# 64 unused bytes in front of the activation tiles: every operand tile of the dense matmuls moves by 64 bytes

## What is computed

```python
x = x + 0.5 * ((silu(h @ w_gate) * (h @ w_up)) @ w_down)      # three times, 1024 x 2816 each
z = h @ w_in + b_in                                            # 1024 x 6672
merged = gates[0] * (attn @ w_proj_attn) + gates[1] * (mlstm @ w_proj_mlstm)
x = x + merged @ w_out
proj = h @ w_in_2                                              # 1024 x 1968
h = h + concat(o_gla, o_mla) @ w_out_2
h = h + (cross attention of h over mem) @ xa_w_o
```

## Time and profile before

| | us |
|---|---|
| median of 3 runs | 1047.71 (1047.59 to 1049.11) |
| profiled execution | 1046.08 |
| its span, from first to last instruction | 1044.4 |
| TensorE (PE) busy | 1011.0, 97% |
| VectorE (DVE) busy | 690.8, 66% |
| ScalarE (ACT) busy | 538.4, 52% |
| GpSimd (POOL) busy | 102.2, 10% |

### The profile page before, as it was taken

The page is one execution under the profiler, slowest core; times in us unless marked ns, Lnnn a source line. Parts: engine busy times, 40 slices in busy tenths (PEclk is TensorE's granted clock), DMA queues, the critical chain, the costliest instruction groups (busy, mean ns, idle before and its releaser), DMA issues.

```text
span 1044.4 us, 20581 instructions
## 1 busy us (share of the span) xinstructions
PE 1011.0 (97%) x8317; PEld 992.4 (95%) x8317; DVE 690.8 (66%) x1084; ACT 538.4 (52%) x779; POOL 102.2 (10%) x66
## 2 busy tenths in 40 slices
PE   6999999999999899999999999999989989999998
PEld 5999999998999799999999999999979889999998
DVE  5766665466869958766666636595566467787642
ACT  4554444244557964455444555485545555444431
POOL 1111110000000100001111104100001012222100
PEclk8999999999999999999999999999999999999999
DMA  8556665554553444565656654344235264655851
GB/s 248 180 178 186 198 221 167 177 162 131 159 196 121 145 138 140 182 223 182 193 168 189 218 193 125 116 123 153 89 104 159 62 202 149 190 184 172 261 171 41
DMA packets 168492, 172.33 MB, mean 165 GB/s; under 512 B 5604, under 2 KB 166894, under 8 KB 168302
## 3 DMA queue, kind: packets, MB, share of 16 engines
q1 hardware_dynamic: 165262, 170.57, 51.4%
q10 hardware_dynamic: 3168, 0.88, 0.5%
HBM read 170.39 MB, written 1.06 MB: 164 GB/s over the span
## 4 chain that ended last, share of the span: by engine, by line
PE 83%; DVE 6%; ACT 5%; issue 4%; DMA 1%; POOL 1%; SPq 0%; ACTq 0%; DVEq 0%; POOLq 0%
PE acc L655 76%; DVE wl L462 2%; DMA raw<-in_ffn_w_gate 1%; ACT wh L443 1%; POOL sq L2545 1%; PE part L992 1%; ACT L1395 0%; PE part L732 0%; PE part L708 0%; PE part L1191 0%; ACT prob L1334 0%; PE part L982 0%; ACT prob L1561 0%; PE part L780 0%; PE part L1173 0%
## 5 line engine op out<-in xcount | busy, mean ns | idle before, releaser
L443 ACT ACTIVATE wh<-raw 128x1024 fp32r<-128x1024 f32 (+3 forms) x298 | 319.4, 1095 | 317.0 <-PE acc L655 189.9
L655 PE MATMUL acc<-ah,wh 128*128 128x256 f32 x1520 | 436.0, 287 | 12.1 <-DVE al L1753 4.1
L462 DVE TENSOR_TENSOR wl<-raw,wh 128x1024 fp32r<-128x1024 f32 (+3 forms) x298 | 391.0, 1351 | 75.8 <-ACT wh L443 72.4
L655 PE MATMUL acc<-ah,wl 128*128 128x256 f32 x1520 | 431.9, 284 | 0.0
L655 PE MATMUL acc<-al,wh 128*128 128x256 f32 x1520 | 431.8, 284 | 0.0
L655 PEld LDWEIGHTS acc<-ah,wh 128*128 128x128 f32 x1520 | 290.1, 191 | 17.5 <-issue 6.9
L655 PEld LDWEIGHTS acc<-ah,wl 128*128 128x128 f32 x1520 | 290.1, 191 | 0.0
L655 PEld LDWEIGHTS acc<-al,wh 128*128 128x128 f32 x1520 | 290.0, 191 | 0.0
L655 PE MATMUL acc<-hh,wh 128*128 128x256 f32 x528 | 148.7, 282 | 0.0
L655 PE MATMUL acc<-hh,wl 128*128 128x256 f32 x528 | 148.6, 281 | 0.0
L655 PE MATMUL acc<-hl,wh 128*128 128x256 f32 x528 | 148.6, 281 | 0.0
(11 more groups left out here) (391 smaller groups left out, 1290.8 us busy)
## 6 DMA issues: line engine op xcount, KB each, us to landing
raw<-in_ffn_w_gate SPq DMA_DIRECT2D x33, 1024.0 KB, 5.3
raw<-in_ffn_w_up SPq DMA_DIRECT2D x33, 1024.0 KB, 5.3
raw<-in_ffn_w_down SPq DMA_DIRECT2D x24, 1408.0 KB, 6.4
raw<-in_w_in SPq DMA_DIRECT2D x33, 1024.0 KB, 5.3
raw<-in_w_out SPq DMA_DIRECT2D x8, 1024.0 KB, 5.2
raw<-in_w_proj_attn SPq DMA_DIRECT2D x4, 1024.0 KB, 5.1
raw<-in_w_proj_mlstm SPq DMA_DIRECT2D x4, 1024.0 KB, 5.7
raw<-in_xa_w_kv SPq DMA_DIRECT2D x4, 1024.0 KB, 5.5
```

The costliest lines, as they stand in the source:

```text
L443: nc.scalar.activation(wh[:, slot, a * nw:b * nw], raw[:, slot, a * nw:b * nw], ACT.Copy).then_inc(S("w_hi"), 1)
L462: nc.vector.tensor_tensor(wl[:, slot, a * nw:b * nw], raw[:, slot, a * nw:b * nw], f(wh[:, slot, a * nw:b * nw]), SUB).then_inc(S("w_lo"), 1)
L655: ins = mm(dst, a, b, start=st and q == 0, stop=en_ and q == 2, skip_group_check=True)
```

## The change

One tile of 16 float32 (64 bytes of each partition) is allocated between `rin` and `ah`. Nothing reads or writes it. The instructions, their order, their shapes and their semaphores stay as they are; every tile that is allocated after it begins 64 bytes later.

```diff
         rs2 = sb("rs2", [P, 2, 4])
         rin = sb("rin", [P, 2, 4])
+        half = sb("half", [P, 16])
         ah = sb("ah", [P, DC, T], f32r)
         al = sb("al", [P, DC, T], f32r)
```

## The result

The changed kernel takes 1020.82 us in the median of 4 runs (1015.89 to 1023.43), the kernel before 1047.65; the ratio is 0.974, with a 95% interval of 0.970 to 0.979. So it is 2.6% faster, and the forecast of no change was wrong. The profiled execution took 1015.89 us, with a span of 1014.2, 30.2 less than before.

What follows compares the result with a forecast made beforehand. TensorE's dense matmuls were taken to bound the kernel, at a rate the 64 bytes would not change. Terms 0 + 0 + 0 + 0 left span 1044.4, profiled execution 1046.1 and median 1047.7 us; range 1045.6 to 1053.7.

Steps and rivals of the forecast that it cites:

- What bounds the kernel: Whole kernel: TensorE, busy 97% of the span; 7,536 dense matmuls at 118.86 ns take 895.7 of 1044.4 us.
- All on the path: Part 2's claim that all 7,536 dense matmuls lie on the path that sets the kernel's time.
- Part 2: Dense matmuls with activations 64 bytes off: cost taken as 0, bounded from float32 rows at 0.4 ns each, 3.0 us.
- Rival (b): Dense matmuls: moving and stationary reads collide at like places of 128-byte blocks; 64 bytes part them, 56.7 us faster, chance 0.10.
- Rival (a): Dense matmuls: moving operand fetched in 128-byte blocks, nine instead of eight; slower, 1053.7 us at the doubled bound, chance 0.17.
- Parts 3 and 4: ScalarE, VectorE and GpSimd work on shifted tiles (3), and DMA loads and stores (4): cost 0 each.
- The range: Median time meant to hold 8 in 10: scatter from 1045.6 us, extended up to 1053.7, with rival (b) left out.
- the doubled bound: Part 2's float32 bound doubled for the faster fp32r stream: 0.8 ns per dense matmul, 6.0 us, giving 1053.7 us.

Runs made afterwards that it cites:

- The run of other forms: TensorE alone, rows of 96 matmuls: fp32r with 64 stationary, 512 or 128 moving columns, and plain float32, at distances 0, 112, 128, 192; plain float32 took 41.72 us at each.
- the last kernel: Against the changed kernel: tiles laid at multiples of 16 bytes, 16 unused bytes ahead of raw, 48 ahead of ah (distance 112); 1016.76 us, 0.9706 to before.

## Why the prediction was wrong

- **What bounds the kernel: right.** The gain came out of the one rate that the prediction put in question, and the chain's long stretch was the right thing to look at. Its stretch of 1,392 takes 158.06 us, where 165.5 was forecast. "All on the path" was too much: the chain before holds some 6,600 of the 7,536 dense matmuls.
- **Part 2, the step that failed: the bound from float32 rows.** It took L834 to L836 and L1191, saw 111.7 and 111.3 ns, and held that an operand off 128 costs or gives nothing. Measured, the rate of the dense matmuls fell from 118.7 to 113.3 ns for most of them and to 117.8 for the others, and the median by 26.8 us. The run of other forms shows plain float32, and fp32r too with 128 moving columns, at one rate at each of the four distances tried; rows 4 and 5 are of float32 with 128 and 129 columns, so they could hardly have shown the effect, in either direction. Doubling the bound for the faster stream did not help, since twice nothing was measured. Their 111.7 and 111.3 ns are per record, moreover, and a float32 matmul leaves two: the 18 are 9 matmuls and the 8 are 4. The question was off too: it asked where one operand starts, and moving both by 64 changes nothing.
- **No row could tell.** All dense matmuls of the kernel before stand at one distance, 128. The text said so ("No fp32r matmul of this trace has an operand off 128") and then bounded below at 0 all the same.
- **Rival (b), two reads in each other's way: right in its direction, and in that the two starts count together,** with a chance of 0.10. Its block of 128 bytes was wrong: with both starts at the same place of 256 bytes (distance 0) the rate is 120.0, not the 118.7 of 128. Its size was mis-sized too: 7.5 ns per matmul, to the 111.3 of float32, where the fast pattern gives 5.3 (118.7 to 113.3) and the slow one 0.9. With all dense matmuls fast, and all on the path, it would have been 7,536 x 5.33 = 40 us; the median gained 26.8. The argument against it, from rows 4, falls with those rows. The Trainium skill ("TensorE: Matmul & The Clock Gate", "Step-by-step: what each phase is for") says that loading the next weights steals no read bandwidth from the running matmul, and the prediction took from it that nothing is left to collide. Measured, the same 1,440 matmuls take 171.15 us with both operands moved by 64 and 163.49 with one of them 64 off, whichever it is. So the two starts do count together; that it is the weight load which holds up the stream, no run shows.
- **Rival (a), blocks of 128 bytes: wrong.** The activations 64 off with the weights 64 off cost nothing (1045.45 us).
- **Parts 3 and 4: right.** DVE and ACT within 0.1 us; the copy into `probT1`, now at a multiple of 128, 590 ns for 592; the store of `res` 2.9 us for 2.8.
- **The range** reached up to the doubled bound and not down, though (b) had found 7.5 ns per matmul that no row explained.

That the two reads clash is still an argument. Shown is that the rate of fp32r matmuls depends on the distance of their two starts, with 256 or 512 moving columns and with 64 stationary ones, and TensorE alone; not with 128 moving columns or in plain float32. The period of 256 bytes and the part of the place were tried in the dense form alone. No run leaves the weight loads out, which would tell a clash with them from another cause.

## What to carry to other kernels

Where fp32r matmuls of 256 or more moving columns bound a kernel, take their rate from the chain and hold it against rows of the same form in a kernel of its own, at several distances of moving to stationary start. Steps of 32 bytes would have missed 112 here; steps of 16, with the stationary operand kept at a multiple of 32, find it. The pad is free as long as there is room. Lay all operand pairs at the same distance; choose on the kernel itself, and time it often, for a distance can have two rates. A rate measured in one form (float32, another width) says nothing about another, and nor does a layout that holds a quantity constant say what changing it would do.

## What the runs showed of the hardware that I had not expected

- Dense fp32r matmuls (128x128 by 128x256, a weight load each) take 113.3 to 129.9 ns by the distance of their two operands in a partition's row, with a period of 256 bytes; most lie at 117 to 122, and 112 bytes with the stationary operand at a multiple of 32 gives 113.3 in TensorE alone (12 rows of 12) and in all long stretches of the last kernel.
- Some distances have two steady rates: 113.3 and 117.8 ns at 64 and 192, in the kernels and in TensorE alone. A stretch keeps its rate for over a thousand matmuls; an interruption can turn it over. The scatter of the changed kernel, 1015.9 to 1029.6 us in eight executions, has this for its main part, as far as the two profiles show.
- The period of the old pattern is five matmuls, 593 ns, whatever the tiles, while the loop has three matmuls to a chunk; a pattern in the starts that does not follow the loop was here the trace of this effect.
